# A trunk layer on one core: the scan's decays from cumulative sums, and three moved steps

## The reference

```python
ada = jnp.dot(jax.nn.silu(c), w_ada) + b_ada          # 2048 -> 6 x 2048
shift1, scale1, gate1, shift2, scale2, gate2 = jnp.split(ada[:, None, :], 6, axis=-1)
h = layer_norm(x) * (1 + scale1) + shift1
z, xbc, dt_raw, q_a, kv_a, k_r, g_logits = jnp.split(jnp.dot(h, w_in), IN_OFFSETS, axis=-1)
y_ssd = ssd_branch(z, xbc, dt_raw, ...)               # conv, silu, scan, gate, rms norm, w_out
y_mla = mla_branch(q_a, kv_a, k_r, ...)               # latent attention, w_mla_out
mix = jnp.dot(g[:, :, 0] * y_ssd + g[:, :, 1] * y_mla, w_mix_out)
x = post_layer_norm(DEEPNORM_ALPHA * x + (1 + gate1) * mix, ln1_g, ln1_b)
h2 = layer_norm(x) * (1 + scale2) + shift2
f = peer_ffn(h2, ...)                                 # top-k of 128*128 experts, rows gathered
return post_layer_norm(DEEPNORM_ALPHA * x + (1 + gate2) * f, ln2_g, ln2_b)
```

```python
def segsum_exp(a):
    cs = jnp.cumsum(a, axis=-1)
    diff = cs[..., :, None] - cs[..., None, :]
    return jnp.exp(jnp.where(mask, diff, -jnp.inf))
```

## Time and profile before

| | us |
|---|---|
| median of 3 runs | 2711.09 (2710.27 to 2713.92) |
| the profiled execution | 2719.48 |
| its span on the core | 2717.0 |
| PE busy | 2374.5 (87%) |
| DVE busy | 2061.6 (76%) |
| ACT busy | 1009.8 (37%) |
| POOL busy | 869.9 (32%) |
| granted TensorE clock, mean | 0.932 of full |

### The profile page before, as it was taken

The page is one execution under the profiler, slowest core; times in us unless marked ns, Lnnn a source line. Parts: engine busy times, 40 slices in busy tenths (PEclk is TensorE's granted clock), DMA queues, the critical chain, the costliest instruction groups (busy, mean ns, idle before and its releaser), DMA issues.

```text
span 2717.0 us, 34317 instructions
## 1 busy us (share of the span) xinstructions
PE 2374.5 (87%) x12532; PEld 1891.1 (70%) x12532; DVE 2061.6 (76%) x2517; ACT 1009.8 (37%) x1428; POOL 869.9 (32%) x733
## 2 busy tenths in 40 slices
PE   4799999999999999999969867666666699999996
PEld 3688877888888887888859857656656664444442
DVE  7777779788888786554576999999999786665577
ACT  2254543344444444433343322227776750000000
POOL 0000011222222221000001566656666454444344
PEclk9799999999999999999989988887787799999998
DMA  9767669566666565555746899999999879999997
GB/s 385 292 215 243 226 228 358 208 213 215 217 217 215 207 215 193 207 189 186 258 178 230 353 419 419 419 419 388 404 407 388 344 256 414 413 413 414 414 413 277
DMA packets 144867, 819.86 MB, mean 302 GB/s; under 512 B 16680, under 2 KB 19360, under 8 KB 70480
## 3 DMA queue, kind: packets, MB, share of 16 engines
q0 software_dynamic: 93200, 477.21, 44.7%
q1 hardware_dynamic: 48480, 335.95, 33.3%
q10 hardware_dynamic: 3040, 4.68, 0.5%
HBM read 813.55 MB, written 4.23 MB: 301 GB/s over the span
## 4 chain that ended last, share of the span: by engine, by line
PE 61%; DVE 23%; DMA 7%; issue 5%; ACT 3%; POOL 1%; ACTq 0%; DVEq 0%; POOLq 0%
PE aux L1155 16%; DVE rrow L2151 9%; PE ps L706 8%; PE ps L707 8%; PE ps L712 7%; PE ps L731 4%; PE ps L732 4%; PE ps L737 4%; DMA rrow<-in_peer_u,acc 3%; DVE acc L1668 2%; DVE rrow_first L2151 1%; DVE wlo L1619 1%; PE aux L992 1%; DMA dskip<-in_D_skip 1%; DMA vden<-in_p_vd 1%
## 5 line engine op out<-in xcount | busy, mean ns | idle before, releaser
L1619 DVE TENSOR_TENSOR wlo<-raw,whi 128x2048 fp32r<-128x2048 f32 x216 | 499.6, 2314 | 292.4 <-ACT whi L1174 281.8
L1174 ACT ACTIVATE whi<-raw 128x2048 fp32r<-128x2048 f32 x216 | 412.1, 1910 | 664.1 <-PE ps L712 386.8
L2236 DVE SCALAR_TENSOR_TENSOR ps<-vrow,acc,ps 128x1024 f32<-128x1024 f32 x231 | 297.5, 1288 | 177.2 <-DMA vrow<-in_p_vg,acc 162.1
L2414 POOL DMA_INDIRECT rrow<-in_peer_u,acc x219 | 354.1, 1617 | 220.3 <-DVE dots L2151 115.2
L2151 DVE CUSTOM_DVE_ANT_0 rrow<-rrow,h 128x2048 f32<-128x2048 f32 x172 | 385.1, 2288 | 16.8 <-DMA rrow<-in_peer_u,acc 16.3
L2414 POOL DMA_INDIRECT vrow<-in_p_vg,acc x256 | 247.4, 966 | 265.3 <-DVE ps L2236 178.0
L2328 POOL DMA_DIRECT2D ada_in<-in_p_ada x128 | 69.3, 542 | 673.2 <-DVEq L1775 529.2
L1096 PE MATMUL aux<-hT,rT 128*128 128x128 f32 x1792 | 233.8, 294 | 37.1 <-ACT rT L1503 37.1
L731 PE MATMUL ps<-h_hi,whi 128*128 128x256 f32 x1040 | 264.6, 295 | 0.0
L1096 PEld LDWEIGHTS aux<-hT,rT 128*128 128x128 f32 x1792 | 226.7, 209 | 46.0 <-issue 31.7
L706 PE MATMUL ps<-whi,h_hi 128*128 128x512 f32 x576 | 235.1, 408 | 24.7 <-ACT whi L1174 24.1
(11 more groups left out here) (361 smaller groups left out, 4337.7 us busy)
## 6 DMA issues: line engine op xcount, KB each, us to landing
raw<-in_p_in SPq DMA_DIRECT2D x104, 1024.0 KB, 4.9
ada_in<-in_p_ada POOLq DMA_DIRECT2D x128, 512.0 KB, 4.8
vden<-in_p_vd SPq DMA_DIRECT2D x64, 1024.0 KB, 8.0
ada_in<-in_p_ada SPq DMA_DIRECT2D x32, 1024.0 KB, 10.1
raw<-in_p_so SPq DMA_DIRECT2D x32, 1024.0 KB, 4.7
raw<-in_p_mo SPq DMA_DIRECT2D x16, 1024.0 KB, 7.2
raw<-in_p_bc SPq DMA_DIRECT2D x16, 1024.0 KB, 6.4
raw<-in_p_mix SPq DMA_DIRECT2D x16, 1024.0 KB, 4.8
```

What stands on the lines that cost most here:

```text
L1174: F(whi[:, n % 2, :, 0:cols_], raw[:, n % 4, :, 0:cols_], ACT.Copy).then_inc(hi_ready, 1)
L1619: V.tensor_tensor(wlo[:, n % 2, :, 0:cols_], raw[:, n % 4, :, 0:cols_], whi[:, n % 2, :, 0:cols_].bitcast(F32), ALU.subtract).then_inc(lo_ ...
L2236: last = V.scalar_tensor_tensor(o, row, w, o, ALU.mult, ALU.add)
L2414: return G.indirect_dma_start(out=dst, out_offset=None, in_=table, in_offset=bass.IndirectOffsetOnAxis(ap=eid_all[:, r:r + 1], axis=0))
```

## The change

It has four parts.

A. *Last modulation quarter.* PE does the rest and the sums of quarter 3 after the first unit of quarter 2 (unit 4), not after the second (unit 5). DVE accumulates chunks 5 to the last of that quarter and adds the bias ahead of the split for unit 5.

B. *Scan decays.* At the start of the MLA output projection PE makes the cumulative sums of all heads with four small matmuls, once with positions on partitions (`cs`) and once with heads on partitions (`csT`). ACT copies both out of PSUM and stores `csT` to a scratch tensor in DRAM (`cs_rows`, 2 stores). In each group POOL waits for the previous group's y, loads two blocks of `cs_rows` broadcast to all partitions into `mt` (512 KB each), waits for them, and in 16 tensor-scalar operations of 128x128 subtracts `cs` and takes the minimum with 0; ACT takes the exponential in place. The decay matmuls on PE, `rad`, and the wait ahead of `cb` go. POOL's loop over groups is unrolled.

C. *Last MLA slab.* Its sum on PE moves from the end of the MLA projection to behind u0 of scan group 0; DVE's row and ACT's store follow it.

D. *Tail.* `TAIL_PE` begins at row 233 instead of 225: 12 rows on PE instead of 16; rows 225, 227, 229 and 231 are added by DVE.

```diff
-        FIRST_PE, TAIL_PE = OHB // 4, range(225, BLK * SEL, 2)
+        FIRST_PE, TAIL_PE = OHB // 4, range(233, BLK * SEL, 2)
...
-                    if q + 1 < QUARTERS:
-                        ada1_rest(q + 1)
-                        ada1_sums(q + 1)
+
+                        if s == (0 if q == QUARTERS - 2 else 1) and q + 1 < QUARTERS:
+                            ada1_rest(q + 1)
+                            ada1_sums(q + 1)
...
-                mm(aux[:, 2, HEADS:2 * HEADS], upper, adt[:, 1, :], start=True, stop=True).then_inc(cum_ready, 1)
+                mm(aux[:, 2, HEADS:2 * HEADS], upper, adt[:, 1, :], start=True, stop=True)
+                for b in range(BLK):
+                    mm(aux[:, 3, b * HEADS:(b + 1) * HEADS], upper, adt[:, b, :], start=True, stop=True)
+                    last = mm(aux[0:HEADS, 1, b * P:b * P + P], adt[:, b, :], upper, start=True, stop=True)
+                last.then_inc(cum_ready, 1)
...
-                pe.wait_ge(row_ready, ADA_MLA + 4)
-                sum_slab(aux[:, 0, :], 1, ADA_MLA + 3)
...
+                            elif q == 0:
+                                pe.wait_ge(row_ready, ADA_MLA + 4)
+                                sum_slab(aux[:, 0, :], 1, ADA_MLA + 3)
                             if q == 2:
...
                                     turn_y(grp)
-                                log_decays((0, 1))
-                            if q == 3:
-                                log_decays((2, 3))
...
-                        pe.wait_ge(decay_exp, grp * 4 + 4)
...
+                F(cs[:, :, :].rearrange("p b h -> p (b h)"), aux[:, 3, 0:BLK * HEADS], ACT.Copy)
+                F(csT[:, :, :].rearrange("h b l -> h (b l)"), aux[0:HEADS, 1, 0:BLK * P], ACT.Copy).then_inc(decay_ready, 1)
+                act.wait_ge(decay_ready, 1)
+                for b in range(BLK):
+                    nc.scalar.dma_start(cs_rows[b * HEADS:(b + 1) * HEADS, :], csT[:, b, :]).then_inc(cs_kept, 16)
...
-                                act.wait_ge(diff_done, grp * 4 + (k + 3))
-                                F(mt[:, k // 2, 4 * (k % 2):4 * (k % 2) + 4, :].rearrange("p h l -> p (h l)"),
-                                  aux[:, 3 - k % 2, :], ACT.Exp).then_inc(decay_exp, 1)
+                                act.wait_ge(diff_ready, grp * 4 + (k + 1))
+                                m = mt[:, k // 2, 4 * (k % 2):4 * (k % 2) + 4, :].rearrange("p h l -> p (h l)")
+                                F(m, m, ACT.Exp).then_inc(decay_exp, 1)
...
-                for s in range(2):
-                    ada1_chunks(q, 4 + s, 5 + s)
-                    lo(U_LOW, 2 * (q - 1) + s, 0, 0)
-                ada1_chunks(q, 6, ADA_V)
+                ada1_chunks(q, 4, 5)
+                lo(U_LOW, 2 * (q - 1), 0, 0)
+                if q < QUARTERS - 1:
+                    ada1_chunks(q, 5, 6)
+                    lo(U_LOW, 2 * (q - 1) + 1, 0, 0)
+                    ada1_chunks(q, 6, ADA_V)
+                else:
+                    ada1_chunks(q, 5, ADA_V)
             mod_quarter(QUARTERS - 1)
+            lo(U_LOW, 2 * (QUARTERS - 2) + 1, 0, 0)
...
+                        pool.wait_ge(y_done, grp + 1)
+                        for b in range(BLK):
+                            G.dma_start(mt[:, b].rearrange("p h l -> p (h l)"),
+                                        cs_rows.rearrange("(b h) l -> b (h l)", b=BLK)[b:b + 1, ds(hd * P, HG * P)]
+                                        .broadcast_to([P, HG * P])).then_inc(cs_in, 16)
+                        pool.wait_ge(cs_in, grp * 32 + 32)
                         for k in range(4):
-                            if k == 2:
-                                ada2(grp + ADA_SSD, 1, True)
-                            pool.wait_ge(diff_done, grp * 4 + (k + 1))
-                            G.tensor_tensor(rad[:, k % 2, :, :], upper.unsqueeze(1).broadcast_to([P, 4, P]),
-                                            adt[:, k // 2, ds(hd + 4 * (k % 2), 4)].unsqueeze(2).broadcast_to([P, 4, P]),
-                                            ALU.mult).then_inc(rad_ready, 1)
+                            for h in range(4 * (k % 2), 4 * (k % 2) + 4):
+                                m = mt[:, k // 2, h, :]
+                                last = G.tensor_scalar(m, m, cs[:, k // 2, hd + h:hd + h + 1], 0.0, ALU.subtract, ALU.min)
+                            last.then_inc(diff_ready, 1)
+                        ada2(grp + ADA_SSD, 1, True)
                         ada2(grp + ADA_SSD, 2, True)
```

More of the change, by code:

```diff
@@ L255, in build @@
         yg = at("yg", 178 * KB, [P, BLK, W])
-        rad = at("rad", 182 * KB, [P, 2, 4, P])
+        csT = at("csT", 142 * KB, [HEADS, BLK, P])
+        cs = sin2
         mt = at("mt", 186 * KB, [P, BLK, HG, P])
@@ L470, in build @@
         xskip_ready = sem("xskip_ready")
-        rad_ready = sem("rad_ready")
+        cs_in = sem("cs_in")
+        diff_ready = sem("diff_ready")
         cb_done = sem("cb_done")
-        cb_read = sem("cb_read")
-        diff_done = sem("diff_done")
+        cs_kept = sem("cs_kept")
         decay_exp = sem("decay_exp")
@@ L552, in build @@
         ada_rows = nc.dram_tensor("ada_rows", (1, ADA_ALL * W), F32, kind="Internal").ap()
+        cs_rows = nc.dram_tensor("cs_rows", (BLK * HEADS, P), F32, kind="Internal").ap()
         x1_kept = nc.dram_tensor("x1_kept", (SEQ, D), F32, kind="Internal").ap()
@@ L750, in _ @@
             pe.sem_inc(pe_used, 2)
-            pe.sem_inc(diff_done, 2)
+            pe.sem_inc(y_done, 1)
             pe.sem_inc(acc_summed, 2)
@@ L941, in ssd_pair @@
                         grp = i * 2 + g
[L943 to L950, removed]
                         for q in range(4):
@@ L1340, in _ @@
                 F(toend[:, :], aux[:, 2, 0:HEADS], ACT.Exp)
-                F(fromst[:, :], aux[:, 2, HEADS:2 * HEADS], ACT.Exp).then_inc(decay_ready, 1)
+                F(fromst[:, :], aux[:, 2, HEADS:2 * HEADS], ACT.Exp)
+                F(cs[:, :, :].rearrange("p b h -> p (b h)"), aux[:, 3, 0:BLK * HEADS], ACT.Copy)
[3 more added lines that the diff above has]
+                    nc.scalar.dma_start(cs_rows[b * HEADS:(b + 1) * HEADS, :], csT[:, b, :]).then_inc(cs_kept, 16)
                 for s in range(4):
@@ L1348, in _ @@
                             ada2_bias(ADA_MLA + s)
-                ada2_store(ADA_MLA + 3)
             def store_y(number, tile):
@@ L1374, in ssd_pair @@
                                 hi(U_SSD, u + k, i, N_SSD)
-                            if k == 3 and not (first and g == 0):
+                            if k == 3:
                                 ada2_store(grp + ADA_SSD - 1)
@@ L1917, in _ @@
                         S.step(V.tensor_tensor(m, ps[:, 1 - s % 2, b, :], m, ALU.mult))
-                ada2_row(aux[:, 0, :], ADA_MLA + 3)
             if on("ssd"):
-                SSD_STEPS = 25 + DC - 1
+                SSD_STEPS = 26 + DC - 1
                 def ssd_pair(i, first):
@@ L1929, in ssd_pair @@
                             lo(U_SSD, u + 2, i, N_SSD)
+                            ada2_row(aux[:, 0, :], ADA_MLA + 3)
                             lo(U_SSD, u + 3, i, N_SSD)
@@ L1966, in ssd_pair @@
                                                upper.unsqueeze(1).broadcast_to([P, 2, P]), ALU.mult))
-                        V.tensor_copy(cbm[:, 2, :], aux[:, 2, 2 * P:3 * P]).then_inc(cb_read, 1)
+                        S.step(V.tensor_copy(cbm[:, 2, :], aux[:, 2, 2 * P:3 * P]))
                         S.wait()
@@ L1977, in ssd_pair @@
                         lo(U_SSD, u + 11, i, N_SSD)
-                        dve.wait_ge(y_done, grp + 1)
+                        dve.wait_ge(y_done, grp + 2)
                         dve.wait_ge(xskip_ready, grp + 1)
@@ L2344, in _ @@
                 pool.wait_ge(pe_used, U_SSD + 2)
-                with pool.Fori(0, 4) as i:
-                    S.enter(i, 4)
+                pool.wait_ge(cs_kept, 16 * BLK)
+                for i in range(4):
                     for g in range(2):
@@ L2375, in _ @@
                         ada2(grp + ADA_SSD, 3, True)
-                S.leave(4)
             if on("mix"):
```

## The result

The changed kernel takes 2762.2 us (2758.95 to 2765.35, 6 runs), the kernel before 2713.55 (2710.27 to 2719.26, 6 runs): a ratio of 1.0173, with a 95% interval of 1.0161 to 1.0184. It is 48.7 us slower. The forecast was slower by 19, with a range that ended at 2748. The direction and the place were right; the size was not.

A forecast was written before the change was run, and what follows sets the result against it. PE looked like the scan's bound, with DVE only just in time (0.2 us of slack). Scan decays +29, MLA start 0, last MLA sum 0, low stage -4.7, tail -5.5 made +19 on 2711: 2730 us, range 2690 to 2748.

The forecast's parts named there:

- The place and the mechanism: Scan groups: POOL issues piece 1 late behind its operations, DVE waits, u6's split is late; +4.2 us a group, +29 in all.
- the landing of the `mt` loads: Scan group start, POOL: both broadcast loads landed 6.3 us after the first issue, with bounds of 5 and 9.
- the fourth rival: Scan groups: `mt` loads land after over 9 us or an operation costs over 1.1; +7 a group, 2750 and up; chance 0.10.
- The price of an operation: POOL's 16 tensor-scalar operations in a scan group: an average of 0.92 us each.
- POOL being held: Scan groups: a POOL operation waits until DVE's operation with two SBUF inputs ends; read from one that took 0.96 us.
- The first rival: Scan groups: POOL isn't held and its operations are short, so piece 1 is on time; -19 us, 2692; chance 0.20.
- the sum by its own steps for a group: Scan groups 1 to 7: piece 1 issued at 715.5 instead of 710.18, PE starts u6 +4.2 us later a group.
- The low stage: Last modulation quarter: sums follow unit 4, so the stage's end at 151.56 becomes 146.9; -4.7 us, bounds -7.4 and -3.
- The MLA start: MLA output projection: four small matmuls and two copies fit into PE's 1.67 us wait; 0, bounds +1 and -3.
- Part C: Last MLA sum behind u0: u0 about 5 us earlier, but POOL holds group 0 as late as before; 0, bounds -8 and +2.
- u0 of the scan at 479: A sign that the forecast is right: u0 of the scan starts at 479.
- The tail: Rows 225 to 231 go to DVE: its add starts 4.2 us earlier, PE has four rows fewer; -5.5, bounds -8 and -3.

The follow-up runs named there:

- Experiment 6: The changed kernel with slab piece 1 issued after the first 8 of POOL's 16 operations instead of after all: 2729.85 us, 1.0052 to the kernel before.
- experiment 7: The changed kernel with the broadcast loads into `mt` issued ahead of the slab's piece 0: 2746.50 us, 1.0124 to the kernel before.
- experiments 5: The changed kernel with 12 tensor-scalar operations a group on POOL instead of 16, a fourth of the decays left out: 2750.24 us, 1.0136 to the kernel before.
- experiment 8: The changed kernel with the `mt` loads ahead of piece 0 and piece 1 issued after 8 of the 16 operations: 2699.06 us, 0.9945 to the kernel before.

## Why the prediction was right in sign and wrong in size

**The place and the mechanism held.** The forecast put the loss on POOL's queue: piece 1 stands behind 16 operations, DVE stands for it, and the split for u6 is too late. The trace shows each link; PE's wait stands before u5 already (9.48 us, where the forecast had some 5), with 0.60 more before u6. Experiment 6, which moves the two issues alone, takes back 32 us: two thirds of the loss, half of the 61 that the decays cost. How rigid the chain behind piece 1 is can be read from four kernels: from DVE's start on piece 1 to the next mark it is 41.50 us in the changed kernel (732.67 to 774.17), 41.55 with twelve operations (726.74 to 768.29), 41.51 with the loads first (722.46 to 763.97) and 41.50 with piece 1 between (719.51 to 761.01). Before it was 42.68 (714.32 to 757.00), of which 0.7 are accumulations that took 3.93 and not 3.22. That an experiment moved the time by less than expected was, in these, decided ahead of that point.

**The step that failed is the landing of the `mt` loads.** I put 6.3 us from the first issue to both landed, "nearer to the first row since the DMA engines are busy 0.62 of this stretch". That share is a mean over a group. At the start of a group two loads of piece 0, two of `mt` and the weight loads come together; the stretch from the `mt` issue to the first operation, in group 3 of the changed kernel:

```profile
701.00:712.00 11.00, 11.00 (x87) 10.00 (x86) 7.79 (x7) 3.77 (x3) 1.19 (x3) 1.00 0.92 330
```

The DMA engines are busy 0.92 of it. The trace of the kernel before had shown as much, had I cut out the 11 us behind its mark, without any load of `mt`:

```profile
688.40:699.40 11.00, 11.00 (x81) 9.52 (x81) 9.05 (x10) 1.91 (x1) 4.23 (x4) 1.00 0.89 307
```

The loads took 11.0 us in group 3 of the changed kernel and 9.65 on average (8.6 of idle time and the 1.05 of the issues), 3.3 more than I had put. The row that showed what a broadcast can take in company was among mine (16.1 in the middle) and made only the fourth rival: loads of over 9 us, +7 a group, 2750 and up, with a chance of 0.10. That rival is what happened, 9.65 us and 7.2 a group. How much of the 9.65 is the broadcast and how much the company stays open; group 0 of experiment 7, 6.8 us with the loads first, shows that the company counts.

**The price of an operation was a smaller miss.** I put 0.92 us, the rows have 1.02: 16 x 0.10 = 1.6 more a group. Free of DVE it is 0.69 to 0.72, not 0.60 or 0.35; beside a working DVE 1.33 in one row of experiment 6. The reading of the earlier trace rows as POOL being held fits these rows. The first rival's estimate by the Trainium skill (GPSIMD Engine Reference, section 3.1) of 0.28 us is far below even the shortest, 0.70; the two rows of experiment 6 agree with the rule of the Trainium skill's SBUF — State Buffer page, "Who interferes with whom".

With these, the sum by its own steps for a group is 4.2 + 3.3 + 1.6 = 9.1; the first issue follows the mark 1.0 us sooner than I had (4.2 against 5.2), and the accumulations take 0.7 less: 7.4, where 7.2 was measured. The 7.2 make 50.6 us for the seven groups instead of 29.

**The low stage was sized too small.** -4.7 was put; the next unit starts 7.2 us earlier, near the bound of -7.4, and alone it gives 6 us at the end. The sums took 6.6 us rather than 8.2, and unit 5 about 7.5 rather than 8.2: I had taken both from rows at a granted clock of 0.64 and 0.65, and they ran at 0.79 and 0.73, means of a part at the lower level and a part at the upper one. Why the lower part was shorter is not shown.

**The MLA start** was put at 0 and the trace has 0.8 us beyond the low stage's gain, within its bounds. **Part C** was put at 0 with the bound of -8 for a POOL that doesn't hold the group. Alone it gives some 3 us; in the changed kernel, where group 0 loses 9.8 us, its mark is 4.8 us early, just the 4.7 that I had for A and C together. That they agree is partly chance: A gave more and group 0 took more. My sign of "u0 of the scan at 479" left out the low stage's own gain (484.1 - 4.7 - 5 is 474); u0 starts at 469.48.

**The tail** was put at -5.5 and gives some 3. DVE's part of it held: -4.2 was put, and with part D alone its adds end 4.0 us earlier from one profile to the other. The rest, for four rows fewer on PE, didn't come: PE stands 4.58 us there before its first row, for nothing that the profile shows.

**The range** ended at 2748, although my own upper bound for the operations alone was +49 for the groups. I had cut it off with the fourth rival, at a chance of 0.10. Of that rival's two conditions the landing alone came true (9.65 us, over 9); the operations stayed under theirs (1.02, not 1.1) and added the smaller part.

## What to carry to other kernels

Before an issue of loads is put behind other work on a queue, find who waits for these loads, and price the work ahead at its worst, beside what the other engines do at that time; moving two issues was worth 32 us here. A mean DMA share over a stage can hide the moment at which several loads are issued together (0.62 and 0.89 in the kernel before): cut out the few microseconds in which the new load would run. And where two limits lie close together, as PE's and DVE's here with 0.2 us between them, taking work off one engine can give nothing until the other's wait is moved too: 2699 against 2701 without that step, 2684 against 2701 with it.

## What was not expected of the hardware

Tensor-scalar operations of 128x128 in a row on POOL took 0.69 us each while DVE stood and 1.33 while it worked, mostly with two SBUF inputs, and on average 1.02 us in the changed kernel, 1.13 in experiments 5 and 7 and 1.2 in experiment 8. Piece 1 of the slab, two loads of 512 KB, took 6.4 to 7.4 us from its issue to DVE's start in the six groups of experiments 5 and 6 where it was issued within 1 us behind a 1 MB weight load, and 4.1 to 5.3 us in the other 22 groups of these two, experiment 7 and the changed kernel, where it was issued 2.3 us or more behind one. No run moved the weight load to show that it is the cause.
